# Scores of two heads in one step: second products over 64 rows on the two halves of the array, and a first query tile 128 columns wide

## What is computed

```python
# branch B: chunked attention with a relative bias (one head)
logits = einsum('qd,kd->qk', q, k) * d ** -0.5 + bias      # masked by chunk
# branch C: forgetting attention (one head), a block of 128 queries
logits = einsum('qd,kd->qk', q, k) * d ** -0.5 + F[q] - F[k] # masked: key <= query
p = softmax(logits);  out = p @ v
```

## Time and profile before

| | before |
|---|---|
| median of 3 runs | 1494.19 us |
| profiled execution, its own time | 1493.45 us |
| its span in the trace | 1491.5 us |
| granted TensorE clock | 0.997 of full |
| PE busy | 1474.0 us, 99% |
| DVE busy | 975.2 us, 65% |
| ACT busy | 666.5 us, 45% |
| DMA | 94 GB/s mean |

### The profile page before, as it was taken

One profiled execution on the slowest core, in us unless ns is written; L12 is line 12 of the kernel. 1 busy time (PEld: TensorE's weight loads), 2 busy tenths in 40 slices (PEclk: granted clock), 3 DMA queues, 4 the chain that ended last, 5 costly groups with the idle time before them and its releaser, 6 DMA issues.

```text
span 1491.5 us, 19540 instructions
## 1 busy us (share of the span) xinstructions
PE 1474.0 (99%) x7022; PEld 1215.7 (82%) x7022; DVE 975.2 (65%) x1614; ACT 666.5 (45%) x1140; POOL 44.8 (3%) x35
## 2 busy tenths in 40 slices
PE   7999999999999999999999999999999999999997
PEld 5888888888888888888878888888888888888886
DVE  5777767565687733776477776675647776357753
ACT  6645555443444422443475555544345443234434
POOL 0000000001100000000200000000030000000001
PEclk9999999999999999999999999999999999999999
DMA  6222212222332233222432222222333322332331
GB/s 230 78 86 78 74 68 72 85 86 85 113 99 98 81 96 120 95 90 76 125 123 85 72 85 77 66 71 79 106 100 98 99 95 77 104 106 98 98 108 63
DMA packets 42561, 139.62 MB, mean 94 GB/s; under 512 B 5364, under 2 KB 5492, under 8 KB 42232
## 3 DMA queue, kind: packets, MB, share of 16 engines
q1 hardware_dynamic: 42192, 138.44, 29.1%
q10 hardware_dynamic: 296, 0.20, 0.1%
HBM read 136.53 MB, written 2.10 MB: 93 GB/s over the span
## 4 chain that ended last, share of the span: by engine, by line
PE 95%; DVE 2%; ACT 1%; DMA 1%; issue 1%; SPq 0%; ACTq 0%; DVEq 0%
PE dense L634 28%; PE dense L636 28%; PE dense L635 28%; PE turned L699 2%; PE branch L726 1%; PE dense L879 1%; PE dense L878 1%; PE dense L877 1%; PE scores L687 1%; PE scores L686 1%; DMA h<-in_x 1%; PE branch L712 1%; DMA raw<-in_w_in 0%; PE scores L690 0%; ACT tmp L1092 0%
## 5 line engine op out<-in xcount | busy, mean ns | idle before, releaser
L634 PE MATMUL dense<-hg,whi 128*128 128x512 f32 x1376 | 547.7, 398 | 4.7 <-DVE hg L1284 4.3
L636 PE MATMUL dense<-hg,wlo 128*128 128x512 f32 x1376 | 537.0, 390 | 0.0
L635 PE MATMUL dense<-hg,whi 128*128 128x512 f32 x1376 | 536.6, 390 | 0.0
L947 ACT ACTIVATE whi<-raw 128x1024 fp32r<-128x1024 f32 (+3 forms) x269 | 265.4, 987 | 441.9 <-PE dense L636 418.0
L1271 DVE TENSOR_TENSOR wlo<-raw,whi 128x1024 fp32r<-128x1024 f32 (+3 forms) x269 | 305.9, 1137 | 185.5 <-ACT whi L947 183.3
L634 PEld LDWEIGHTS dense<-hg,whi 128*128 128x128 f32 x1376 | 259.3, 188 | 60.8 <-issue 4.3
L636 PEld LDWEIGHTS dense<-hg,wlo 128*128 128x128 f32 x1376 | 258.6, 188 | 55.0
L635 PEld LDWEIGHTS dense<-hg,whi 128*128 128x128 f32 x1376 | 259.1, 188 | 51.7 <-issue 1.2
L634 PE MATMUL dense<-act,whi 128*128 128x512 f32 x528 | 207.2, 392 | 0.0
L636 PE MATMUL dense<-act,wlo 128*128 128x512 f32 x528 | 205.6, 389 | 0.0
L635 PE MATMUL dense<-act,whi 128*128 128x512 f32 x528 | 205.5, 389 | 0.0
(11 more groups left out here) (188 smaller groups left out, 1270.9 us busy)
## 6 DMA issues: line engine op xcount, KB each, us to landing
raw<-in_w_up SPq DMA_DIRECT2D x88, 512.0 KB, 3.5
raw<-in_w_gate SPq DMA_DIRECT2D x48, 512.0 KB, 3.5
raw<-in_w_in SPq DMA_DIRECT2D x35, 512.0 KB, 3.5
raw<-in_w_down SPq DMA_DIRECT2D x32, 384.0 KB, 3.0
raw<-in_w_out SPq DMA_DIRECT2D x16, 512.0 KB, 3.5
raw<-in_w_down SPq DMA_DIRECT2D x16, 320.0 KB, 2.9
raw<-in_w_down_last SPq DMA_DIRECT2D x10, 512.0 KB, 3.5
raw<-in_w_br_a SPq DMA_DIRECT2D x8, 512.0 KB, 3.5
```

The costliest lines, as they stand in the source:

```text
L634: mm(out, a, xhi, start=start, stop=False)
L635: mm(out, a, xlo, start=False, stop=False)
L636: return mm(out, b, xhi, start=False, stop=stop)
L947: fn(whi[:, s, 0:cols], raw[:, r, 0:cols], ACT.Copy).then_inc(w_hi.sem, 1)
```

## The change

Slots with s = 1 no longer issue scores. A slot with s = 0 waits for both banks and issues the scores of both heads: first the two products with the high keys over 128 rows, then the two with the low keys, each over only the 64 rows of the head's high queries (head 0 on rows 0 to 63, head 1 on rows 64 to 127), then in branch C the two forget products. The low-by-low term is no longer in the sum. The columns are those of the tile, so 128 for t = 0. Nothing changes on the other engines, in the transposes, or in the probability-by-value products.

```diff
-                w = width(i)
+                if s == 1:
+                    return
+                n = width(i)
                 scores_free(l, i)
+                scores_free(l, i + 1)
...
-                b = bank_s[i % 2]
-                n = max(w, 2 * P)
-                a, kk = q_st[p][:, s, t * P:(t + 1) * P], k_st(kc, s)
-                mm(b[:, 0:n], a, kk[:, 0, k0:k0 + n], start=True, stop=False)
-                last = mm(b[:, 0:n], a, kk[:, 1, k0:k0 + n], start=False, stop=not forget)
+                rows = slice(t * P, (t + 1) * P)
+                for s in range(2):
+                    mm(bank_s[s][:, 0:n], q_st[p][:, s, rows], k_st(kc, s)[:, 0, 0:n], start=True, stop=False)
+                for s in range(2):
+                    r = slice(s * HD, (s + 1) * HD)
+                    last = mm(bank_s[s][:, 0:n], q_st[p][r, s, rows], k_st(kc, s)[r, 1, 0:n],
+                              start=False, stop=not forget)
+                    if not forget:
+                        last.then_inc(scores.sem, 1)
                 if forget:
-                    f = 2 * (p - A_PAIRS - B_PAIRS) + s
-                    last = mm(b[:, 0:n], fq[:, f, t * P:(t + 1) * P], fk[:, 0:n], start=False, stop=True)
-                last.then_inc(scores.sem, 1)
+                    for s in range(2):
+                        f = 2 * (p - A_PAIRS - B_PAIRS) + s
+                        mm(bank_s[s][:, 0:n], fq[:, f, rows], fk[:, 0:n],
+                           start=False, stop=True).then_inc(scores.sem, 1)
```

More of the change, by code:

```diff
@@ L673, in step_scores @@
                 p, t, s = STEPS[i]
-                w = width(i)
+                if s == 1:
+                    return
+                n = width(i)
                 scores_free(l, i)
+                scores_free(l, i + 1)
                 kc = p - 3
-                k0 = 0
                 forget = p >= A_PAIRS + B_PAIRS
-                if s == 0 and t == 0:
+                if t == 0:
                     pe.wait_ge(qk_lo.sem, qk_lo.at(l, QK_AT[p - 1] - 1))
```

## The result

The changed kernel takes 1502.65 us in the median of 5 runs (1501.55 to 1503.99), against 1494.19 us (1493.65 to 1495.51, 5 runs) before: 8.46 us more, ratio 1.0056 with a 95% interval of 1.0044 to 1.0069. The forecast was 1502.7 us. Its profiled execution took 1502.26 us, 8.81 over that of before.

What follows compares the result with a forecast made beforehand. The prediction took PE to bound the kernel: 12.0 us of mode changes less 5.2 saved gives +6.8, plus 1.7 of waits is +8.5 us on 1494.19, so 1502.7 us. The range was 1499.3 to 1507.7.

Steps and rivals of the forecast that it cites:

- The ways in and out: On PE, each group changes array mode twice, costing 0.35 us in branch B and 0.40 in C: 12.0 us.
- The saving by pairs: The two 64-row products of a group run together, saving one product's time: 4.1 us for t = 3, 2, 1.
- The 128-column products: At t = 0, products of 128 columns take 0.11 us each, the weight load's pace: 1.1 us gained.
- The moved wait: PE waits in slot 38 for DVE's maximum of step 37: 0.86 us a layer, 1.7 us in all.
- slot 46: The next closest place for PE to wait on DVE's maximum: a stall of 0.0 to 0.1 us.
- The slip of DVE's maximum in slot 36: Slot 36's first scores come later, so DVE's maximum and its gapless run slip by about 0.35 us.
- (2): Rival: 128-column products at t = 0 fall back to four passes, 0.214 us each; +11.8 us, 1506.0; chance 0.25.
- (3): Rival: the 64-row halves, or only their loads, do not run together; 1506.2 to 1507.7 us; chance 0.12.
- (4): Rival: 64-row halves stay in the 128-row mode, so mode changes are free; -3.5 us, 1490.7; chance 0.08.
- (5): Rival: at mode changes the loads hide and only the 0.09 us gaps stay; +2.3 us, 1496.5; chance 0.08.
- (1): The forecast itself: mode changes at full price, halves together, 128 columns at the load's pace; 1502.7 us; chance 0.42.

Runs made afterwards that it cites:

- x4: Kernel before, one head per slot, but each second product over its head's 64 rows alone and 128 columns for t = 0: 1515.58 us, ratio 1.0144.
- x8: Changed kernel with the 64-row pair issued three times in a row in each group: 1512.55 us, one run.
- x6: Changed kernel with branch C's forget products ahead of the 64-row pair: 1503.01 us, one run.
- x1: Kernel before with 128 instead of 256 columns for t = 0, heads and slots as before: 1493.74 us, ratio 0.9997.
- x2: Changed kernel with the second products over all 128 rows instead of 64-row halves: 1496.07 us, ratio 1.0013.
- x7: Changed kernel with the wait for head 1's bank moved behind head 0's first product: 1502.15 us, one run.
- x3: Changed kernel with 256 columns for t = 0, as in the kernel before: 1503.04 us, ratio 1.0061.

## Why the prediction was right, point by point

**The ways in and out: right.** Forecast 0.20 in, 0.15 out ahead of transposes and 0.20 ahead of forget products, read off four products over 4 rows. Found (changed kernel): 0.09 to 0.10 ahead of the pair and 0.11 behind it, 0.09 again, and 0.11 or 0.06 for the next load. The price does not depend on the number of rows (4 or 64) nor on whether one half works or both (x4). It is paid per visit (x8). That the larger part of each way is the load that nothing covers is an inference from its size, from its place behind the first pair (x8) and from x6; no run took the load away by itself.

The Trainium skill's rule that a change of tiling mode drains TensorE ("TensorEngine Tiling (Array Packing)", Key Properties) holds here, with 0.09 us for the gap. That page's "up to 2x" (Theoretical Speedup) holds too, but within the mode only: x8's 64 further pairs.

**The saving by pairs: right.** 4.1 us for t = 3, 2, 1. Net of the ways, the groups of 256 and 384 columns cost 0.23 to 0.25 and 0.21 us in branch B, 0.30 and 0.24 in C, where 0.23, 0.18, 0.28 and 0.23 were forecast. These are the shifts of the dense products from just ahead of a group to just ahead of the next one, changed kernel against before.

**The 128-column products: half right.** The term that was off is the gain at t = 0: the prediction has 1.1 us, from 0.11 us for each of "3 product times" in B and "5" in C, and the changed kernel shows 2.1. As a stream they do come every 0.112 us (x1, x2), which fits the bound by the load. But the bound holds between two successive products only. The first one behind a dense product goes at 0.057, so does the pair, and so does the first forget product (0.164 = 0.057 + 0.107 for the load already counted as way out). In the changed kernel that makes 2 such in a B group and 3 in a C group, some 0.05 each. The eight t = 0 groups cost 0.9 us net of all where 1.9 were forecast: 1.0 us too many. x1's expectation, written after the changed kernel's trace was seen, made the opposite error and took the 0.057 for the pace.

**The moved wait: right in place and cause, a little small.** 0.86 us a layer forecast for slot 38, 0.90 found; slot 46 "0.0 to 0.1", found 0.05. Together 1.9 us for the 1.7 in the sum. The slip of DVE's maximum in slot 36, "about 0.35", is in the rows: it starts at 236.34 instead of 233.32, while PE's slot 36 starts at 234.87 instead of 232.19, so 0.34 of the 3.02 are the slip, and DVE then runs without a gap up to the maximum of step 37. x2 shows the same wait without a 64-row product. x7 names the bank.

**The sum.** 8.5 forecast, 7.97 in the stretches, 8.46 between the medians. The 1.0 us too many at t = 0 are partly made up by 0.2 of waits and some 0.3 spread over the other groups, 0.2 of it at 384 columns. So that the stretches come within 0.5 us of the forecast is in part luck, and that the median hit it to 0.1 us is luck altogether; that the ways, the pairs and the wait have the sizes they were given is not. One bound was added up wrongly: ways at 0.30 a group and stalls of 0.5 give 9.6 - 5.2 + 1.0 = 5.4, so the range should start at 1499.6 and not at 1499.3. It changes nothing.

**The rivals.** (2), four passes, fell by the rows of x1. (That the reduced form takes one pass is read from this trace, 0.227 us against 0.86 for 512 columns; the section that the prediction cites there states only the four passes of true float32.) (3), the halves one after the other, fell by the 0.003 us between their starts and by x8. (4) and (5), ways that are free or cost only the gaps, fell by the distances in each group. All of them were told from (1) by the distances between starts, none by the durations of the records.

**No better version.** x1_cols is the only one under the kernel before, by 0.8 us in the stretches, which its 11 runs do not tell from nothing (ratio 0.9988 to 1.0006). Without the mode changes (x2) the change is still slower, for its wait.

## What to carry to other kernels

Two products on halves of the array save one product's time per visit and pay 0.35 to 0.40 us for the visit. On this chip one pair of 512-column products (0.23 us) does not pay for that; by an estimate from these numbers it takes two such pairs in a visit, or four of 256 columns (0.12 us each). Look in the trace for any place where the row or column mode already changes, and read the distances between starts there: four products over 4 rows gave this price before anything was built. And when two steps are merged, ask which wait of the second one comes a step early, and look where the engine waited for is busy without a gap at that moment; its mean load does not show it.

## What the runs showed of the hardware

- The distance of 128-column fp32r products is 0.057 us for the first behind a dense product and 0.112 for each next one (x1, x2). 256 columns take 0.116 and 512 take 0.227. From 256 columns to 128 a stream gains only 0.004 us a product; no width between them was run.
- No fallback to four passes (0.214 us) was seen for fp32r at 128 columns: in a stream they stand 0.11 to 0.12 us apart (x1, x2).
- From the last 128-row product of 128 columns to the pair are 0.205 us (214.20 to 214.41), and 0.21 with 256 columns (x3): the width of that product hardly matters there.
- Going from 128 rows to the 64-row pair, or back, leaves a gap of 0.09 to 0.10 us, and the product behind the first one of the new mode is late by another 0.11 (0.06 for a transpose). The two halves start 0.003 to 0.004 us apart.
- Inside the 64-row mode the third pair of 512 columns starts 0.23 us behind the second, loads of both halves included (x8).
